# Retention's output products in high and low float32r parts, its gated product on VectorE, and convolution taps moved to a later stage

## The chip, the cores and the metric

One core of a Trainium2 chip runs the whole program. The metric is the device time in microseconds of one execution, as the median of several runs. The engines have short names in the profile: PE is TensorE (matmuls), PEld its weight loads, DVE VectorE, ACT ScalarE, POOL GpSimd, SP the engine that issues most transfers.

## The reference, cut to what matters

Three mixers follow each other over 256 tokens of width 1024: a gated delta rule, a short convolution, and a third block. The third block projects its normed input by one wide matrix into queries and keys (1024 each), values and a gate (2048 each), and the inputs of a convolution of width 31. What this case touches, in float32:

```python
# retention, per head h of 4 (dk 256, dv 512), chunks of 128 tokens
scores = einsum('bhid,bhjd->bhij', qc, kc) * decay_mask
inner  = einsum('bhij,bhje->bhie', scores, vc)
...
ret = head_groupnorm(retention_chunkwise(qh, kh, vh)).reshape(B, S, RET_V_DIM)
y_a = (ret * silu(z_ret)) @ w_ret_out
a = u_val * sigmoid(u_gate)
a = causal_depthwise_conv_2(a, conv_w, conv_b)      # 31 taps
a = silu(layernorm(a, conv_ln_g, conv_ln_b))
y_b = (a * silu(z_conv)) @ w_conv_out
merged = sigmoid(g_a) * y_a + sigmoid(g_b) * y_b
```

With 256 tokens there are two chunks, and the kernel computes the second chunk's sum over both chunks' keys directly, without a state.

## The kernel before

**Stages.** The program is one chain of projections, each cut into chunks of 256 weight columns (PHASES): ... qk (8 chunks), v (8), zret (8, the retention's gate), zconv (4), gates (8), ret_out (8), conv_out (4), w_out (4). A weight chunk of 128x2048 float32 is loaded into one of four raw slots; ScalarE writes its high part (w_hi, float32r, in halves of 128x1024), VectorE the rest (w_lo = raw - w_hi), and TensorE multiplies high x high, high x low and low x high (wide_half, L727, L728 and L734: eight matmuls with w_hi, then four with w_lo per half, of 512 columns each). There are four places for halves of w_hi and w_lo, so a half can be split only when TensorE has finished the half that stood there four halves earlier.

**Who does what beside.** Each engine has one fixed program order. For each chunk VectorE first does two low splits (second half of the next chunk, first half of the one after), then what `each` gives it: a number of convolution taps (conv_share, instructions of 128x256, L2399, L2396 for a first tap), and the work of the stage. There are 8 x 31 = 248 taps; conv_share takes from a list in order and does nothing when the list is empty. The conv_share counts for each chunk are written by hand.

- glu: 3, 4, 5, 4, 2, 4 taps from chunk 2 on; qk: 3 for each chunk.
- v: TensorE computes one head's scores after each of the first four chunks (`scores`, L1134); VectorE multiplies them with the decay into st (L2459); ScalarE copies v out of PSUM after each second chunk (vt, L1641).
- zret: after each chunk TensorE computes one output block of 128 tokens x 512 from st and vt (`weighted_sums`, L1146, and L1148 for the second chunk of tokens), as float32 matmuls. VectorE takes statistics from it (L2477, L2481); ScalarE the root (L1656) and then the normed output og (L1662). GpSimd multiplies og with the silu of the gate, back into vt (L1773).
- zconv: TensorE transposes the product (`turn_two`, L1160), ScalarE and VectorE write its high and low parts (yT_hi, yT_lo).
- gates: ScalarE takes sigmoids (L1641). VectorE has taps and, behind them in its last chunk, two sums of the convolved channels for the layer norm's mean (L2502, L2506). GpSimd makes two sums before those (L1777, and L1780, which waits for cv_step of 186 taps).
- ret_out: after its first chunk TensorE waits for those sums (`layer_norm`, ln_sum_step of 4) and multiplies them with ones (L1169). VectorE and ScalarE do the norm beside the later chunks.

Of the kernel before, what the change touches and what calls it, by code (L numbers as in the profile page):

```python
# [53 lines left out]
PHASES = [("qkv", 16), ("z", 8), ("gdn_out", 8), ("sc_in", 32), ("sc_out", 8), ("glu", 8), ("qk", 8), ("v", 8),  # L54
          ("zret", 8), ("zconv", 4), ("gates", 8), ("ret_out", 8), ("conv_out", 4), ("w_out", 4)]
ORDER = [name for name, _ in PHASES]
READ_BY = {name: "act" if name in ("z", "v", "zret", "zconv", "gates") else "dve" for name in ORDER}
DEEP = ("gdn_out", "sc_out", "ret_out")
DEEP_NEXT = ("sc_in", "glu")
CW2 = 2 * CC  # L60
# [30 lines left out]
V_PRE, V_PRE2, V_BADA, V_CB, V_LG, V_LB, V_C, V_SC = 0, 16, 24, 48, 56, 64, 72, 80  # L91
ANGLE_STEPS = 12
SHIFTED = ((4, 5, 6, 7), (6, 7))
E_LEAST = 0.5 * math.log(RMS_EPS) - 0.1
EYE, T_SIDE, S_BASE = 3, 4, 5
G_ROW = 32
# [2 lines left out]
def build(nc, x_in, pre_norm_w, post_norm_w, gdn_w_in, gdn_conv_w, gdn_A_log, gdn_dt_bias, gdn_norm_w, gdn_w_out,  # L99
# [3 lines left out]
    with ctx:  # L103
# [123 lines left out]
        qkT = at("qkT", o_q, [P, 2 * KT, SEQ])  # L227
        vt = at("vt", o_q + 16 * K, [P, NT, 2 * D])
        o_t = o_q + 32 * K
        st = at("st", o_t, [P, RH, 3 * P])  # L230
        glu, rp1, rp2 = (at(n, o_t + 2 * s * K, [P, 2, SEQ]) for s, n in enumerate(("glu", "rp1", "rp2")))
        lnm = at("lnm", o_t + 7 * K, [P, 2, SEQ])
        cT_hi, cT_lo = at("cT_hi", o_ar, [P, KT, SEQ], F32R), at("cT_lo", o_q + 24 * K, [P, KT, SEQ], F32R)
# [16 lines left out]
        def bank(b, inner=SEQ):  # L250
# [64 lines left out]
        cv_step, mean_done, xc_ready, a2_ready, var_done, ln_step = (  # L315
            sem(n) for n in ("cv_step", "mean_done", "xc_ready", "a2_ready", "var_done", "ln_step"))
        lna_ready, lns_ready, lnz_ready = sem("lna_ready"), sem("lns_ready"), sem("lnz_ready")
        chi_ready, cop_ready, mg_ready, mhi_ready, mop_ready = (
            sem(n) for n in ("chi_ready", "cop_ready", "mg_ready", "mhi_ready", "mop_ready"))
        qs_done, o1_ready, gn_rec, ln_scalars = (  # L320
            sem(n) for n in ("qs_done", "o1_ready", "gn_rec", "ln_scalars"))
        mg_turned = sem("mg_turned")
# [256 lines left out]
        def _(pe):  # L579
# [558 lines left out]
            def weighted_sums(c):  # L1138

                h, t = c // NT, c % NT  # L1140
                pe.wait_ge(st_ready, min(RH, c + 1))
                if c >= 4:
                    pe.wait_ge(gn_ready, c - 3)
                vh = slice(h * RDV, (h + 1) * RDV)
                o = psum[:, 4 + c % 4, :]
                mm = pe.matmul(o, st[:, h, t * P:(t + 1) * P], vt[:, 0, vh], start=True, stop=(t == 0))  # L1146
                if t:
                    mm = pe.matmul(o, st[:, h, SEQ:SEQ + P], vt[:, 1, vh], start=False, stop=True)  # L1148
                mm.then_inc(ro_done, 1)
            wide_phase("zret", hT_hi, hT_lo, beside=weighted_sums)  # L1150

# [57 lines left out]
        def _(act):  # L1209
# [434 lines left out]
            def channels_out(dst, func):  # L1644
# [1 line left out]
                    act.wait_ge(half_done, done)  # L1646
                    act.activation(dst[:, bass.ds(i * 8 + 2 * j, 2), :], bank(j), func).then_inc(bank_free, 1)
                return each
            chunks("v", tokens_out(vt, ACT.Copy))
            z_ret = tokens_out(zr, ACT.Silu)  # L1650

            def group_norm(h):
# [36 lines left out]
            def layer_norm(i, j, done):  # L1689
                c = 4 * i + j  # L1690
                if c == 1:
                    for q in range(KT // 2):
                        pair = slice(2 * q, 2 * q + 2)
                        act.wait_ge(xc_ready, q + 1)
                        act.activation(a2[:, pair, :], cv[:, pair, :], ACT.Square).then_inc(a2_ready, 1)
                if c == 3:
                    act.wait_ge(var_done, 1)
                    act.activation(lnm[:, 1, :], psum[:, 7, 0:SEQ], ACT.Sqrt, scale=1.0 / D, bias=eps_n[:, :]).then_inc(ln_step, 1)
                if c in (4, 5):
                    for n in range(KH2 * (c - 4), KH2 * (c - 3)):  # L1700
                        act.wait_ge(lns_ready, n // 2 + 1)
                        act.activation(cv[:, n, :], cv[:, n, :], ACT.Silu, scale=par[:, 1, V_LG + n:V_LG + n + 1],
                                       bias=par[:, 1, V_LB + n:V_LB + n + 1]).then_inc(lna_ready, 1)
                if c in (5, 6):
                    for q in range(2 * (c - 5), 2 * (c - 4)):
                        pair = slice(2 * q, 2 * q + 2)
                        act.wait_ge(lnz_ready, q + 1)
                        act.activation(cT_hi[:, pair, :], cv[:, pair, :], ACT.Copy).then_inc(chi_ready, 1)
            chunks("ret_out", layer_norm, unroll=True)
            act.activation(warm[:, 1:2], eps_r[:, :], ACT.Sqrt)  # L1710

# [16 lines left out]
        @block.gpsimd  # L1728
        def _(pool):
            pool.memset(ba_raw[:, :, :], 0.0).then_inc(padded, 1)  # L1730
            pool.memset(Tq[:, :], 0.0).then_inc(filled, 1)
            pool.wait_ge(small_loaded, SMALL)
            pool.wait_ge(small_ready, 3)
            pool.tensor_scalar(keep[:, :], const[:, C_LOW, :], -1.0, 1.0, ALU.mult, ALU.add).then_inc(filled, 1)
            pool.wait_ge(filled, 1)
            pool.memset(Tq[:, 0:BS * BS:BS + 1], 1.0).then_inc(filled, 1)
            pool.wait_ge(filled, EYE)
            def mask(n):
                p, c = n // NT, n % NT
                mine = PT[:, c, HG * p:HG * (p + 1), :]  # L1740
                pool.wait_ge(pt_ready, n + 1)
                pool.tensor_tensor(mine, mine, heads(keep[:, :], HG), ALU.mult).then_inc(masked, 1)
            for n in range(LATE):
                mask(n)
            pool.wait_ge(l2_sum, KT)
            pool.wait_ge(qkv_ready, COUNT["qkv"])
            pool.memset(Tc[0:BS, :, BS:2 * BS], 0.0).then_inc(filled, 1)
            pool.wait_ge(ktok_ready, KT // 2)
            pool.memset(S[0], 0.0).then_inc(filled, 1)
            pool.wait_ge(lo_ready, 2 * (FIRST["z"] + 7))  # L1750
            pool.memset(S[1], 0.0).then_inc(filled, 1)
            pool.wait_ge(eg_ready, 1)
            pool.wait_ge(ktok_ready, KT // 2)
            for p in range(NPAIR):
                for n in {0: (4, 5), 1: (6, 7)}.get(p, ()):
                    mask(n)
                if p == 0:
                    pool.wait_ge(half_done, 4 + 2 * FIRST["gdn_out"])
                else:
                    pool.wait_ge(s1_done, p)  # L1760
                for a in range(HG):
                    h = HG * p + a
                    i = pool.tensor_scalar(kdec[:, a, :], ktok[:, h // 2, :], wdec[:, h:h + 1], None, ALU.mult)
                i.then_inc(kdec_ready, 1)

            pool.wait_ge(yT_turned, KT)
            pool.memset(ada_sum[:, :, :], 0.0).then_inc(ada_used, ADA)

            for n in range(NT * RH):
                h, t = n // NT, n % NT  # L1770
                pool.wait_ge(gn_ready, n + 1)
                vh = slice(h * RDV, (h + 1) * RDV)
                pool.tensor_tensor(vt[:, t, vh], og[t][:, :], zr[:, t, vh], ALU.mult).then_inc(rg_ready, 1)  # L1773

            pool.wait_ge(rg_ready, NT * RH)
            pool.wait_ge(cv_step, CW * 4)
            pool.tensor_tensor(ln_sum[0][:, :, :], cv[:, 0:2, :], cv[:, 2:4, :], ALU.add).then_inc(ln_sum_step, 1)  # L1777
            pool.wait_ge(ln_sum_step, 1)
            pool.wait_ge(cv_step, CW * 6)
            pool.tensor_tensor(ln_sum[0][:, :, :], ln_sum[0][:, :, :], cv[:, 4:6, :], ALU.add).then_inc(ln_sum_step, 1)  # L1780
# [3 lines left out]
        def _(dve):  # L1784
# [668 lines left out]

            def decayed(i, j, done):
                c = 4 * i + j
                conv_share(9 if c < RH else 8)
                if c < RH:
                    dve.wait_ge(sco_done, c + 1)
                    dve.tensor_tensor(st[:, c, :], psum[:, 4 + c, 0:3 * P], decay[:, c, :], ALU.mult).then_inc(st_ready, 1)  # L2459
            dve.wait_ge(decay_loaded, 16)  # L2460
            dve.wait_ge(bank_free, 4 + FIRST["v"])
            chunks("v", decayed, unroll=True)

            def group_scale(h):
# [2 lines left out]
                dve.wait_ge(gn_rec, 2 * h + 1)  # L2467
                dve.scalar_tensor_tensor(out=gnm[:, :], in0=gmv[:, :, 0], scalar=-1.0, in1=grs[:, :], op0=ALU.mult, op1=ALU.mult).then_inc(gn_rec, 1)

            def group_norm(i, j, done):  # L2470
                n = 4 * i + j
                h, t = n // NT, n % NT
                if n and t == 0:
                    group_scale(h - 1)
                conv_share(7)
                dve.wait_ge(ro_done, n + 1)
                dve.bn_stats(gst[:, t, :], psum[:, 4 + n % 4, :]).then_inc(gn_step, 1)  # L2477
                dve.wait_ge(gn_step, 2 * n + 1)
                if h:
                    dve.wait_ge(gn_rec, 2 * h)  # L2480
                dve.bn_aggr(gmv[:, t, :], gst[:, t, :]).then_inc(gn_step, 1)  # L2481
            chunks("zret", group_norm, unroll=True)

            def turned_pairs(i, j, done):
                if j == 0:
                    group_scale(RH - 1)
                conv_share(5 if j else 8)
                split_two(j)

            def split_two(q):  # L2490
# [26 lines left out]
            def layer_norm(i, j, done):  # L2517
# [27 lines left out]
                if c in (6, 7):  # L2545
                    for q in range(2 * (c - 6), 2 * (c - 5)):
                        pair = pairs[q]
                        dve.wait_ge(chi_ready, q + 1)
                        part_lo(cT_lo[:, pair, :], cv[:, pair, :], cT_hi[:, pair, :]).then_inc(cop_ready, 1)
                if j == 3:  # L2550
                    dve.wait_ge(half_done, done)
# [85 lines left out]
```

## Time and profile before

| | |
|---|---|
| median of 3 runs | 838.21 us (837.5 to 838.33) |
| profiled execution, own time | 837.87 us |
| its span, first to last instruction | 836.1 us |
| PE busy | 827.8 us (99%) |
| DVE busy | 731.1 us (87%) |
| ACT busy | 500.2 us (60%) |
| POOL busy | 45.4 us (5%) |

Read it so: the share of an engine says how much of the span it has an instruction at work. Starts in a timeline are microseconds from the start of the span. Matmuls are pipelined, so the distance of two starts, not the duration, is what one costs.

### The profile page before, as it was taken

The numbers are of one execution on the slowest core, as the hardware profiler recorded it, in microseconds if no ns is written. First come the engines' busy times: TensorE is split into PE (matmuls) and PEld (weight loads), VectorE is DVE, ScalarE is ACT, GpSimd is POOL, SyncE is SP. The second block draws the span as 40 slices with busy tenths as digits, with TensorE's granted clock in tenths as the row PEclk, the third lists the DMA queues.
The fourth block names the chain that finished last, engine by engine and source line by source line (L and its number), as shares of the span: only waits on it lengthen the run. The fifth ranks groups of instructions, "written<-read, shape, count | busy, mean of one in ns | idle before, by whom it ended". The sixth has DMA issues, their size and how long they took to land.

```text
span 836.1 us, 13942 instructions
## 1 busy us (share of the span) xinstructions
PE 827.8 (99%) x5146; PEld 725.1 (87%) x5146; DVE 731.1 (87%) x1179; ACT 500.2 (60%) x804; POOL 45.4 (5%) x46
## 2 busy tenths in 40 slices
PE   8999999999999999999999999999999999999997
PEld 8999998789888888888888788998887798888886
DVE  7799899868877898888989979999999999988774
ACT  6899858576566555555565775333346675546743
POOL 0001101341100000000000000000001220000000
PEclk9999999999999999999999999999999999999999
DMA  9875675511875877777776656655454435564531
GB/s 277 256 253 169 211 245 174 146 38 45 278 232 179 261 262 263 257 256 252 238 257 218 221 185 213 202 184 169 155 198 151 152 118 200 186 231 171 188 115 50
DMA packets 129882, 164.13 MB, mean 196 GB/s; under 512 B 17407, under 2 KB 92199, under 8 KB 129703
## 3 DMA queue, kind: packets, MB, share of 16 engines
q1 hardware_dynamic: 129831, 163.45, 59.9%
q8 instruction: 33, 0.54, 0.3%
q14 instruction: 18, 0.15, 0.1%
HBM read 159.20 MB, written 4.23 MB: 195 GB/s over the span
## 4 chain that ended last, share of the span: by engine, by line
PE 98%; DVE 1%; DMA 1%; issue 0%; ACT 0%; DVEq 0%; SPq 0%; ACTq 0%
PE psum L695 16%; PE psum L727 14%; PE psum L728 14%; PE psum L734 14%; PE psum L704 8%; PE psum L677 6%; PE psum L686 6%; PE psum L678 6%; PE psum L1028 2%; PE psum L631 1%; PE psum L641 1%; PE psum L635 1%; PE psum L1033 1%; PE psum L915 1%; PE psum L1146 1%; PE psum L1134 1%
## 5 line engine op out<-in xcount | busy, mean ns | idle before, releaser
L1220 ACT ACTIVATE w_hi<-w_raw 128x1024 fp32r<-128x1024 f32 x255 | 266.6, 1061 | 188.2 <-PE psum L734 87.1
L1786 DVE TENSOR_TENSOR w_lo<-w_raw,w_hi 128x1024 fp32r<-128x1024 f32 x256 | 305.2, 1221 | 44.3 <-ACT w_hi L1220 42.2
L695 PE MATMUL psum<-hT,w_hi 128*128 128x512 f32 x576 | 138.9, 391 | 0.0
L695 PEld LDWEIGHTS psum<-hT,w_hi 128*128 128x128 f32 x576 | 105.4, 188 | 20.2
L727 PE MATMUL psum<-w_hi,hT 128*128 128x512 f32 x280 | 113.3, 405 | 0.0
L728 PE MATMUL psum<-w_hi,hT 128*128 128x512 f32 x280 | 109.3, 390 | 0.0
L2399 DVE SCALAR_TENSOR_TENSOR cv<-aP,par,cv 128x256 f32<-128x256 f32 x240 | 107.9, 519 | 0.0
L677 PE MATMUL psum<-hT,w_hi 128*128 128x256 f32 x432 | 107.4, 286 | 0.0
L678 PE MATMUL psum<-hT,w_hi 128*128 128x256 f32 x432 | 105.9, 283 | 0.0
L677 PEld LDWEIGHTS psum<-hT,w_hi 128*128 128x128 f32 x432 | 82.8, 192 | 0.4 <-issue 0.2
L678 PEld LDWEIGHTS psum<-hT,w_hi 128*128 128x128 f32 x432 | 82.9, 192 | 0.3 <-issue 0.2
L704 PEld LDWEIGHTS psum<-hT,w_lo 128*128 128x128 f32 x576 | 74.8, 191 | 3.3
L704 PE MATMUL psum<-hT,w_lo 128*128 128x256 f32 x576 | 76.1, 283 | 0.0
L727 PE MATMUL psum<-w_hi,yT_hi 128*128 128x512 f32 x192 | 75.8, 395 | 0.0
L734 PE MATMUL psum<-w_lo,hT 128*128 128x512 f32 x280 | 75.6, 390 | 0.0
L728 PE MATMUL psum<-w_hi,yT_lo 128*128 128x512 f32 x192 | 74.8, 390 | 0.0
L727 PEld LDWEIGHTS psum<-w_hi,hT 128*128 128x128 f32 x280 | 52.6, 188 | 12.0 <-issue 1.7
L728 PEld LDWEIGHTS psum<-w_hi,hT 128*128 128x128 f32 x280 | 52.6, 188 | 12.0 <-issue 1.7
L734 PEld LDWEIGHTS psum<-w_lo,hT 128*128 128x128 f32 x280 | 52.6, 188 | 11.2
L686 PE MATMUL psum<-hT,w_lo 128*128 128x256 f32 x432 | 60.6, 283 | 0.0
L686 PEld LDWEIGHTS psum<-hT,w_lo 128*128 128x128 f32 x432 | 55.7, 192 | 0.0
L734 PE MATMUL psum<-w_lo,yT_hi 128*128 128x512 f32 x192 | 52.7, 389 | 0.0
(341 smaller groups left out, 1108.6 us busy)
## 6 DMA issues: line engine op xcount, KB each, us to landing
w_raw<-in_w_in_dram SPq DMA_DIRECT2D x44, 1024.0 KB, 5.1
w_raw<-in_sc_w_in_dram SPq DMA_DIRECT2D x32, 1024.0 KB, 7.9
w_raw<-in_gdn_w_in_dram SPq DMA_DIRECT2D x23, 1024.0 KB, 7.1
ada<-in_w_ada_dram SPq DMA_DIRECT2D x24, 512.0 KB, 4.8
w_raw<-in_gdn_w_out_dram SPq DMA_DIRECT2D x8, 1024.0 KB, 5.5
w_raw<-in_sc_w_out_dram SPq DMA_DIRECT2D x8, 1024.0 KB, 6.4
w_raw<-in_w_ret_out_dram SPq DMA_DIRECT2D x8, 1024.0 KB, 5.1
w_raw<-in_w_conv_out_dram SPq DMA_DIRECT2D x4, 1024.0 KB, 5.1
```

What stands on the lines that cost most here:

```text
L677: pe.matmul(o[:, m, :], w_hi[s][:, k, mine], a_hi[:, ka, :], start=m == 0 and ka == 0, stop=False, skip_group_check=True)
L678: pe.matmul(o[:, m, :], w_hi[s][:, k, mine], a_lo[:, ka, :], start=False, stop=False, skip_group_check=True)
L686: mm = pe.matmul(o[:, m, :], w_lo[s][:, k, mine], a_hi[:, ka, :], start=False, stop=ka == KT - 1, skip_group_check=True)
L695: pe.matmul(o, w_hi[s][:, k, mine], hT[:, h * KH2 + k, :, :], start=h == 0 and k == 0, stop=False, skip_group_check=True)
L704: mm = pe.matmul(o, w_lo[s][:, k, mine], hT_hi[:, ka, :], start=False, stop=ka == KT - 1, skip_group_check=True)
L727: pe.matmul(psum[:, b + m, :], a_hi[:, ka, mine], wide(w_hi[s])[:, e, :], start=start and h == 0 and e == 0, stop=False, skip_group_check= ...
L728: pe.matmul(psum[:, b + m, :], a_lo[:, ka, mine], wide(w_hi[s])[:, e, :], start=False, stop=False, skip_group_check=True)
L734: mm = pe.matmul(psum[:, b + m, :], a_hi[:, k + 2 * h + e, mine], wide(w_lo[s])[:, e, :], start=False, stop=stop and h == 1 and e == 1, sk ...
L1028: mm = pe.matmul(b[:, a, :], left(a), right(a), start=True, stop=True)
L1220: act.activation((w_hi[half_slot(g, h)] if home is None else third_hi[half_slot(g, home)])[:, :, :], raw[slot][:, h * KH2:(h + 1) * KH2, : ...
L1786: return dve.tensor_tensor(o, whole, hi.bitcast(F32), ALU.subtract)
L2399: dve.scalar_tensor_tensor(out=cv[:, n, :], in0=src, scalar=w, in1=cv[:, n, :], op0=ALU.mult, op1=ALU.add).then_inc(cv_step, 1)
```

## The change

TensorE's output products use st and vt as high and low float32r parts, three products in place of one float32 product. In v, ScalarE writes the high parts of vt (from PSUM) and of st, VectorE the low ones, and VectorE frees v's banks. VectorE, not GpSimd, multiplies og with the gate (`gated`), one head late in program order. Taps: in v from 9 and 8 for each chunk to 8, then 6, 6, 6 and 7; in zret from 7 to 6. conv_share in gates is as before: 4 for chunk 0, 10 for each other. The semaphore chi_ready is renamed part_hi_ready and counts these parts first.

```diff
-READ_BY = {name: "act" if name in ("z", "v", "zret", "zconv", "gates") else "dve" for name in ORDER}
+READ_BY = {name: "act" if name in ("z", "zret", "zconv", "gates") else "dve" for name in ORDER}
+PARTS_BY = [sum((d >= RH) + d % 2 for d in range(c + 1)) for c in range(COUNT["v"])]
...
+        vt_hi, vt_lo = at("vt_hi", o_q + 16 * K, [P, NT, 2 * D], F32R), at("vt_lo", o_yT + 16 * K, [P, NT, 2 * D], F32R)
+        st_hi, st_lo = (at(n, o_q + 6 * s * K, [P, RH, 3 * P], F32R) for s, n in enumerate(("st_hi", "st_lo")))
...
             def weighted_sums(c):
-                pe.wait_ge(st_ready, min(RH, c + 1))
+                pe.wait_ge(st_ready, RH + h + 1)
...
-                mm = pe.matmul(o, st[:, h, t * P:(t + 1) * P], vt[:, 0, vh], start=True, stop=(t == 0))
-                if t:
-                    mm = pe.matmul(o, st[:, h, SEQ:SEQ + P], vt[:, 1, vh], start=False, stop=True)
+                for b in range(t + 1):
+                    cs = slice(t * P, (t + 1) * P) if b == 0 else slice(SEQ, SEQ + P)
+                    pe.matmul(o, st_hi[:, h, cs], vt_hi[:, b, vh], start=b == 0, stop=False, skip_group_check=True)
+                    pe.matmul(o, st_hi[:, h, cs], vt_lo[:, b, vh], start=False, stop=False, skip_group_check=True)
+                    mm = pe.matmul(o, st_lo[:, h, cs], vt_hi[:, b, vh], start=False, stop=b == t, skip_group_check=True)
...
# ScalarE
-            chunks("v", tokens_out(vt, ACT.Copy))
+            def beside_v(i, j, done):
+                c = 4 * i + j
+                if c >= RH:
+                    act.wait_ge(st_ready, RH)
+                    act.wait_ge(sco_done, RH)
+                    act.activation(st_hi[:, c - RH, :], st[:, c - RH, :], ACT.Copy).then_inc(part_hi_ready, 1)
+                if c % 2:
+                    act.wait_ge(half_done, done)
+                    act.activation(vt_hi[:, :, c // 2 * CW2:(c // 2 + 1) * CW2], psum[:, j - 1:j + 1, :], ACT.Copy).then_inc(part_hi_ready, 1)
+            chunks("v", beside_v, unroll=True)
...
# GpSimd
-            for n in range(NT * RH):
-                h, t = n // NT, n % NT
-                pool.wait_ge(gn_ready, n + 1)
-                vh = slice(h * RDV, (h + 1) * RDV)
-                pool.tensor_tensor(vt[:, t, vh], og[t][:, :], zr[:, t, vh], ALU.mult).then_inc(rg_ready, 1)
...
# VectorE, v
-                conv_share(9 if c < RH else 8)
+                conv_share(8 if c < RH else 6 + c // 7)
...
+                else:
+                    dve.wait_ge(part_hi_ready, PARTS_BY[c - 1] + 1)
+                    part_lo(st_lo[:, c - RH, :], st[:, c - RH, :], st_hi[:, c - RH, :]).then_inc(st_ready, 1)
+                if c % 2:
+                    dve.wait_ge(part_hi_ready, PARTS_BY[c])
+                    columns = slice(c // 2 * CW2, (c // 2 + 1) * CW2)
+                    part_lo(vt_lo[:, :, columns], psum[:, j - 1:j + 1, :], vt_hi[:, :, columns]).then_inc(bank_free, 2)
...
# VectorE, zret and zconv
+            def gated(h):
+                vh = slice(h * RDV, (h + 1) * RDV)
+                for t in range(NT):
+                    dve.wait_ge(gn_ready, NT * h + t + 1)
+                    dve.tensor_tensor(vt[:, t, vh], og[t][:, :], zr[:, t, vh], ALU.mult).then_inc(rg_ready, 1)
...
-                conv_share(7)
+                conv_share(6)
...
+                if n and t == 0:
+                    gated(h - 1)
...
                 conv_share(5 if j else 8)
+                if j == 0:
+                    gated(RH - 1)
                 split_two(j)
```

## Rows read from the trace of the kernel before

**Rows 1.** Page, busy us, share of the span, instructions.
```profile
PE 827.8 (99%) x5146; PEld 725.1 (87%) x5146; DVE 731.1 (87%) x1179; ACT 500.2 (60%) x804; POOL 45.4 (5%) x46
```

**Rows 2.** Page, chain that ended last, shares by engine.
```profile
PE 98%; DVE 1%; DMA 1%; issue 0%; ACT 0%; DVEq 0%; SPq 0%; ACTq 0%
```

**Rows 3.** Busy time in stretches: v, zconv, gates.
```profile
core 0: us, PE busy (x) PEld busy (x) DVE busy (x) ACT busy (x) POOL busy (x), PEclk, DMA share, GB/s
567.40:616.60 49.20, 49.20 (x228) 41.08 (x227) 47.34 (x88) 19.73 (x19) 0.00 (x0) 1.00 0.53 171
...
670.80:697.20 26.40, 26.40 (x226) 26.40 (x224) 26.33 (x43) 18.25 (x25) 5.57 (x4) 1.00 0.49 160
697.20:740.80 43.60, 43.60 (x195) 36.12 (x193) 43.60 (x80) 21.76 (x22) 0.00 (x0) 1.00 0.52 170
```

**Rows 4.** Timeline of PE in zret: start us, us, engine, line, operation.
```profile
622.05 1.02 PE L1146 MATMUL psum<-vt,st 128*128 128x512 f32 x2
...
625.67 0.39 PE L727 MATMUL psum<-w_hi,hT 128*128 128x512 f32 x1
...
628.40 1.02 PE L1146 MATMUL psum<-vt,st 128*128 128x512 f32 x2
...
632.88 0.39 PE L727 MATMUL psum<-w_hi,hT 128*128 128x512 f32 x1
```

**Rows 5.** Timeline of DVE: decay multiply in v, first part of zret.
```profile
576.37 0.55 DVE L2459 TENSOR_TENSOR st<-psum,decay 128x384 f32<-128x384 f32 x1
...
619.49 2.41 DVE L1786 TENSOR_TENSOR w_lo<-w_raw,w_hi 128x1024 fp32r<-128x1024 f32 x2
```

**Rows 6.** Timeline of POOL: one pair of multiplies, second layer-norm sum.
```profile
637.10 2.88 POOL L1773 TENSOR_TENSOR vt<-og,zr 128x512 f32<-128x512 f32 x2 [415.67 <-ACT og L1662]
...
694.84 1.33 POOL L1780 TENSOR_TENSOR ln_sum<-ln_sum,cv 128x512 f32<-128x512 f32 x1 [11.33 <-DVE cv L2399]
```

**Rows 7.** Timeline of DVE: taps and splits in zret, a product in ret_out.
```profile
636.12 4.94 DVE L2399 SCALAR_TENSOR_TENSOR cv<-aP,par,cv 128x256 f32<-128x256 f32 x7
...
641.80 2.33 DVE L1786 TENSOR_TENSOR w_lo<-w_raw,w_hi 128x1024 fp32r<-128x1024 f32 x2
644.04 2.85 DVE L2399 SCALAR_TENSOR_TENSOR cv<-aP,par,cv 128x256 f32<-128x256 f32 x7
...
655.83 2.33 DVE L1786 TENSOR_TENSOR w_lo<-w_raw,w_hi 128x1024 fp32r<-128x1024 f32 x2
...
776.60 1.29 DVE L2544 TENSOR_TENSOR cv<-cv,zc 128x512 f32<-128x512 f32 x2
```

**Rows 8.** Timeline of DVE in gates, from its part for chunk 1 on.
```profile
706.74 2.35 DVE L1786 TENSOR_TENSOR w_lo<-w_raw,w_hi 128x1024 fp32r<-128x1024 f32 x2
709.01 4.04 DVE L2399 SCALAR_TENSOR_TENSOR cv<-aP,par,cv 128x256 f32<-128x256 f32 x10
...
737.87 2.37 DVE L1786 TENSOR_TENSOR w_lo<-w_raw,w_hi 128x1024 fp32r<-128x1024 f32 x2
...
742.81 0.70 DVE L2502 TENSOR_TENSOR ln_sum<-ln_sum,cv 128x512 f32<-128x512 f32 x1
743.54 0.42 DVE L2506 TENSOR_TENSOR ln_sum<-ln_sum 128x256 f32<-128x256 f32 x1
```

**Rows 9.** Timeline of PE: chunk 1 of gates, its second half, the mean matmul.
```profile
702.74 0.39 PE L727 MATMUL psum<-w_hi,hT 128*128 128x512 f32 x1
...
705.46 0.39 PE L727 MATMUL psum<-w_hi,hT 128*128 128x512 f32 x1
...
746.26 0.59 PE L1169 MATMUL psum<-ln_sum,const 128*128 128x256 f32 x2
```

**Rows 10.** Timeline of ACT in gates.
```profile
705.72 1.06 ACT L1220 ACTIVATE w_hi<-w_raw 128x1024 fp32r<-128x1024 f32 x1 [1.72 <-PE psum L734]
```

**Rows 11.** Stretches behind the last matmul, columns as in rows 3.
```profile
831.00:832.00 1.00, 0.14 (x2) 0.00 (x0) 1.00 (x4) 0.77 (x3) 0.00 (x0) 1.00 0.46 174
...
834.00:834.50 0.50, 0.00 (x0) 0.00 (x0) 0.00 (x0) 0.00 (x0) 0.00 (x0) 0.52 0.98 365
```

More of the change, by code:

```diff
@@ L317, in build @@
         lna_ready, lns_ready, lnz_ready = sem("lna_ready"), sem("lns_ready"), sem("lnz_ready")
-        chi_ready, cop_ready, mg_ready, mhi_ready, mop_ready = (
-            sem(n) for n in ("chi_ready", "cop_ready", "mg_ready", "mhi_ready", "mop_ready"))
+        part_hi_ready, cop_ready, mg_ready, mhi_ready, mop_ready = (
+            sem(n) for n in ("part_hi_ready", "cop_ready", "mg_ready", "mhi_ready", "mop_ready"))
         qs_done, o1_ready, gn_rec, ln_scalars = (
@@ L1707, in layer_norm @@
                         act.wait_ge(lnz_ready, q + 1)
-                        act.activation(cT_hi[:, pair, :], cv[:, pair, :], ACT.Copy).then_inc(chi_ready, 1)
+                        act.activation(cT_hi[:, pair, :], cv[:, pair, :], ACT.Copy).then_inc(part_hi_ready, 1)
             chunks("ret_out", layer_norm, unroll=True)
@@ L2547, in layer_norm @@
                         pair = pairs[q]
-                        dve.wait_ge(chi_ready, q + 1)
+                        dve.wait_ge(part_hi_ready, 2 * RH + q + 1)
                         part_lo(cT_lo[:, pair, :], cv[:, pair, :], cT_hi[:, pair, :]).then_inc(cop_ready, 1)
```

## The prediction, made before the change was run

> **What bounds the kernel now.** I read the page's busy times first: the matmuls cover 99% of the span [rows 1]. The chain that ended last says the same: 98% of it is PE [rows 2]. So only two things can move the time: matmul work that is taken off TensorE, and a wait that TensorE does not have today. The table by stage shows no PE idle in v (from 567.4), zconv and gates (to 740.8), at a granted clock of 1.00, its 2.4 GHz level, while VectorE (DVE) is full too in zconv and gates: 26.33 of 26.40 us and 43.60 of 43.60 [rows 3]. The timelines of single engines then show how late DVE runs behind PE, and where. That distance decides this case. I call the start of DVE's part for a chunk minus PE's start of that chunk its lag.
>
> **What the change takes from TensorE.** Today each of the 12 output products is a full float32 matmul, recorded as two. A weight half of 12 matmuls takes 628.40 - 625.67 = 2.73 us, 0.2275 each; with one float32 product it takes 625.67 - 622.05 = 3.62, with two 632.88 - 628.40 = 4.48 [rows 4]. So a head (three products) costs 0.89 + 1.75 = 2.64 us, four heads 10.56. Afterwards a head is nine high/low products of the same shape and kind as the weight matmuls: 9 x 0.2275 = 2.05, four heads 8.19. TensorE gains 2.4 us, all on the chain. Nothing else on TensorE changes. Bounds of this term: 2.3 by the dearer pair alone (12 x (0.875 - 0.6825)) and 2.5 by the single (12 x (0.89 - 0.6825)).
>
> **The v stage.** ScalarE's copy of v stays and writes the high part; it gets four more copies, of 128x384. A copy of 1024 columns takes it 1.06 us [rows 10], so one of 384 less than that, and it idles 29 of the 49 us there [rows 3]: no cost. DVE gets four st_lo (128x384, priced as today's decay multiply, 0.55 long and some 0.46 from start to next start [rows 5]) and four vt_lo (128x1024, one input in PSUM; priced as a weight split of that shape, 1.14 from start to next start [rows 8]; a PSUM input may make it dearer or cheaper by a tenth, within the lag's reserve below), 6.4 us in all, and loses 11 taps of 0.396 [rows 8], 4.4 us. Its lag at the end of v, 619.49 - 616.6 = 2.9 today [rows 5], grows to about 4.4 us. What hides this: each DVE part begins with the low half that PE wants 5.44 + 2.72 + 1.82 = 9.98 us after the chunk's start, and the split takes 1.2, so PE waits only once the lag passes 8.8 (the three terms are a chunk, a half and eight matmuls of [rows 4]). The banks of v are freed by DVE instead of ScalarE, a few us later, but PE comes back to a pair only a pair of chunks (over 10 us) afterwards. What the first product newly waits for, st_lo of head 0, is written in DVE's part for chunk 4 of v, four chunks before PE reaches it at 622.05 [rows 4]. No PE wait here; if the cover were gone, each us would count in full.
>
> **zret and zconv.** GpSimd's eight multiplies go. While a pair of them runs (2.88 us from 637.10), seven DVE taps take 4.94 us in place of 2.85 [rows 6, 7]: 2.09 us lost, four times, 8.4 in all. DVE now does the multiplies itself: 128x512 with both inputs in SBUF, two in 1.29 [rows 7], 4.9 in all, and 8 taps (3.2) leave. The Trainium skill (GPSIMD Engine Reference, Key points) says that GpSimd shares its SBUF interfaces with VectorE and that instructions with two SBUF inputs contend; the 4.94 against 2.85 agrees. By rows a pair of DVE parts costs 655.83 - 641.80 = 14.03 today [rows 7] and 14.03 - 2.09 - 0.79 + 1.22 = 12.4 after, against 13.52 - 0.6 = 12.9 for PE. So DVE, which falls behind today, catches up, down to the least lag that the weight slots allow. In zconv its part (8 or 5 taps as today) is 5.45 against 6.6 for PE, so it catches up there as well. Today its lag at chunk 1 of gates is 706.74 - 702.74 = 4.0 [rows 8, 9]; by this walk it is at the least that the slots allow. This gain cannot reach PE: PE waits for none of it.
>
> **gates: where the taps land.** The shares must add up to 248 taps (8 blocks of channels, 31 taps). Before: 22 (glu) + 24 (qk) + 68 (v) + 56 + 23 leaves 55 for gates: 4, five times 10, 1, 0. After: 22 + 24 + 57 + 48 + 23 leaves 74: 4 and seven times 10. So chunks 6 and 7 of gates, in which DVE recovers today, are full. A part with 10 taps takes 6.23 us (706.74 to 737.87 is five of them) [rows 8]; PE's chunk takes 5.44. And behind the last tap stand the two sums of the layer norm (742.81 to 743.96, 1.15 us), for which PE waits after the first chunk of ret_out. Today they are ready 2.3 us before PE reaches that matmul at 746.26 [rows 8, 9].
>
> Step by step, with PE 2.4 us earlier. PE starts chunk 1 of gates at 702.74 - 2.4 = 700.35. The second split in DVE's part for it needs ScalarE's high copy, which needs the slot of PE's half (today PE 705.46, copy 705.72 to 706.78) [rows 9, 10]; so it starts at 704.4 at the earliest, however early DVE is. Plus 1.14 and 3.95 for ten taps: 709.5. GpSimd's second layer-norm sum waits for tap 186, which is now the eighth of this part. It lasts 1.33 us [rows 6], and a multiply pair of 2.88 costs DVE 2.09, 73% of its length: +1.0, 710.5. Six more parts of 6.23: 747.9. The two sums: 749.0. PE arrives at 746.26 - 2.4 = 743.9 and waits **5.2 us**. It goes on at 749.1, where today it goes on at 746.26: **+2.8 us**. All behind it (the rest of ret_out, conv_out, w_out) is PE-bound and shifts with it. Before the wait, the lag at chunk 7 is 741.6 - 733.0 = 8.6, just inside 8.8, so a low half may hold PE for a few tenths already; that would be part of the same 5.2. Bounds: if GpSimd's sum pushes nothing and the slots hold nothing back, DVE's work alone gives 700.35 + 1.2 + 7 x 6.23 + 1.15 = 746.3, no change at all. If DVE enters with today's lag of 4.0 at chunk 1, 700.35 + 4.0 + 43.6 + 1.15 + 1.0 = 750.1, +3.8.
>
> **The clock behind the wait.** After its last matmul (end 831.14) TensorE is idle and the granted clock goes from 1.00 to 0.50, which is 1.2 GHz, at 834.0, 2.9 us later [rows 11]. A wait of 5.2 us is longer than that. No row shows how long it then stays down once work resumes. Below: no cost, if it does not fall. Above: it stays down for a whole chunk's work, 5.44 us lost. I take the time it took to fall, 2.9 us at half speed, as an estimate: 1.45 us lost. The Trainium skill (TensorE: Matmul & The Clock Gate, Part 1) states that an idle array goes to the lower clock and needs sustained work to return; the tail agrees on the fall, and no run here shows the return.
>
> **The cases.** The sum is made on the profiled execution, span 836.1, own time 837.87; the median of the runs is 838.21, 0.3 above it, and I add differences to the median.
> - Late sums, clock falls: 838.2 + 2.8 + 1.45 = **842.5**. Chance 0.49.
> - Late sums, clock holds (the fall may also come later than in the tail): 841.0 (to 842.0 with the larger lag). Chance 0.31.
> - Rival on the other side, the sums are not late: 838.2 - 2.4 = 835.8. It decides if DVE is done by 743.9. For it: DVE gets 3.5 us back in zret and zconv. Against it: those us end at the slot limit, and even at the bound DVE ends at 746.3; its parts in gates would have to be 5 us cheaper than the rows. Chance 0.06.
> - The two cancel, at the bound of no push and no hold: 838.2. Chance 0.06.
> - DVE is later than walked, because the new steps of v and zret (low parts waiting for ScalarE, multiplies waiting for the normed output) add to the lag, or the clock stays low for long: about 845 or more. Chance 0.08.
>
> A measurement of this kernel tells about 0.2% (1.7 us) from no change. The range 840.0 to 844.5 holds the first two cases, 0.8. Faster 0.06, same 0.07 (the cancelling case and the edge of the second), slower 0.87.
>
> **What the profile after would show.** Right: 36 products at 0.23 us, zret shorter by 2.4; groups of taps in zret no longer stretched; seven parts of 6.23 us back to back in gates; a PE wait of about 5 us on DVE's ln_sum in front of the layer norm's mean matmul, and granted clock under 1.00 around it. Wrong: no PE wait there (then the tap or split price or the count of taps is off), or a PE wait on w_lo, on a bank in v, or on st_lo. A stall of the right size with the clock at 1.00 would take away the 1.45.

## The result: 0.6% slower, and the profile after

The changed kernel takes 843.0 us (median, 842.28 to 844.61) against 838.17 for the one before: a ratio of 1.0061, 95% interval 1.0048 to 1.0074. The execution shown below took 844.11 us itself, 1.1 above its median, with a span of 842.3 against 836.1. This is the page's chain of work that ended last, which answers to [rows 2]:

```profile
PE 83%; DVE 9%; DMA 3%; issue 2%; ACT 1%; SPq 0%; DVEq 0%; ACTq 0%
```

PE had 98% of it before. Now DVE has 9%. Some 5 of these 9 are the 44.6 us from 705.16 to 749.76 in gates, where the chain runs through DVE's splits and taps. Nearly all of the rest, and of DMA's 3%, lies before 440 us, in sc_out and ahead of it: the chain gets there through the small wait of L730 below, and that has nothing to do with the change. Who waited for whom on PE (us in total, times, longest) names the place:

```profile
PE psum L1174 <- DVE ln_sum L2532: 5.0, 1, 5.0
...
PE psum L730 <- ACT w_hi L1225: 0.3, 1, 0.3
```

L1174 is the matmul for the layer norm's mean. The first row did not exist before. The second is a weight half that came late in sc_out, long before the changed stages, in this execution; the kernel of the seventh experiment shows such a row too (0.5) and the first experiment's does not.

PE's timeline, first an output product of zret (answers to [rows 4]), then the place of the wait (answers to [rows 9]):

```profile
622.89 0.39 PE L1151 MATMUL psum<-vt_hi,st_hi 128*128 128x512 f32 x1
623.12 0.39 PE L1152 MATMUL psum<-vt_lo,st_hi 128*128 128x512 f32 x1
623.35 0.39 PE L1153 MATMUL psum<-vt_hi,st_lo 128*128 128x512 f32 x1
623.57 0.39 PE L730 MATMUL psum<-w_hi,hT 128*128 128x512 f32 x1
...
743.70 1.07 PE L737 MATMUL psum<-w_lo,yT_hi 128*128 128x512 f32 x4
749.81 1.22 PE L1174 MATMUL psum<-ln_sum,const 128*128 128x256 f32 x2 [5.04 <-DVE ln_sum L2532]
750.47 0.99 PE L730 MATMUL psum<-w_hi,yT_hi 128*128 128x512 f32 x1
751.26 0.63 PE L731 MATMUL psum<-w_hi,yT_lo 128*128 128x512 f32 x1
751.68 0.63 PE L730 MATMUL psum<-w_hi,yT_hi 128*128 128x512 f32 x1
...
755.69 0.40 PE L730 MATMUL psum<-w_hi,yT_hi 128*128 128x512 f32 x1
```

Three products start 0.227 us apart, in 0.68 us together. PE would start the mean matmul at 743.70 + 4 x 0.227 = 744.61. It starts 5.20 us later, and then matmuls of 512 columns follow at 0.43 us instead of 0.23 until 755.69. From the first output product to the point where PE reaches the mean matmul it is 744.61 - 622.89 = 121.72 us, before 746.26 - 622.05 = 124.21 [rows 4, 9]: TensorE did gain 2.49 us.

DVE's timeline in gates (answers to [rows 8]):

```profile
705.16 1.23 DVE L1795 TENSOR_TENSOR w_lo<-w_raw,w_hi 128x1024 fp32r<-128x1024 f32 x1 [1.49 <-ACT w_hi L1225]
706.30 3.25 DVE L2408 SCALAR_TENSOR_TENSOR cv<-aP,par,cv 128x256 f32<-128x256 f32 x8
709.47 1.71 DVE L2405 TENSOR_SCALAR cv<-aP,par 128x256 f32<-128x256 f32 x2
711.10 2.35 DVE L1795 TENSOR_TENSOR w_lo<-w_raw,w_hi 128x1024 fp32r<-128x1024 f32 x2
...
742.26 2.35 DVE L1795 TENSOR_TENSOR w_lo<-w_raw,w_hi 128x1024 fp32r<-128x1024 f32 x2
744.54 4.03 DVE L2408 SCALAR_TENSOR_TENSOR cv<-aP,par,cv 128x256 f32<-128x256 f32 x10
748.61 0.69 DVE L2528 TENSOR_TENSOR ln_sum<-ln_sum,cv 128x512 f32<-128x512 f32 x1
749.33 0.43 DVE L2532 TENSOR_TENSOR ln_sum<-ln_sum 128x256 f32<-128x256 f32 x1
```

Read it from the top. In its part for chunk 1 DVE idles 1.49 us for ScalarE's high copy: it is not behind here, it is held. From 705.16 on it never idles again. The row of L2405 holds two taps; GpSimd's second sum (1.33 us from 709.69) runs beside them and stretches them. Five parts take 742.26 - 711.10 = 31.16 us, 6.23 each; the last ten taps and the sums end at 749.76, and PE goes on at 749.81.

Busy time by stretch around the wait (columns as in [rows 3]; the figure behind POOL's is the granted clock):

```profile
747.00:748.00 1.00, 0.00 (x0) 0.00 (x0) 1.00 (x3) 0.00 (x0) 0.00 (x0) 1.00 1.01 393
748.00:749.00 1.00, 0.00 (x0) 0.00 (x0) 0.97 (x3) 0.00 (x0) 0.00 (x0) 0.76 0.11 43
...
754.00:755.00 1.00, 1.00 (x4) 0.81 (x3) 0.00 (x0) 0.00 (x0) 0.00 (x0) 0.50 1.04 403
755.00:756.00 1.00, 1.00 (x5) 0.77 (x5) 0.00 (x0) 0.05 (x1) 0.00 (x0) 0.83 1.06 371
```

The clock is at 0.50 (1.2 GHz) from about 748.5 to about 755.3 (0.76 is about half of its stretch, 0.83 two thirds of one). Work at that level from 749.81 to 755.3 loses half of 5.5 us, 2.75. The timeline agrees: from the mean matmul to the next half it is 755.69 - 749.81 = 5.88 us, and in the kernel before 749.46 - 746.26 = 3.20, 2.7 less. The difference of the two spans then comes out: -2.49 (products) + 0.84 (PE reaches the first product at 622.89, not 622.05) + 5.20 (the wait) + about 2.7 (the clock) = 6.2, and 842.3 - 836.1 is 6.2. The 0.84 is there before v begins (PE starts v at 568.47, not 567.62), ahead of everything that was changed. It belongs to these two executions: the medians differ by 4.8, and less the 5.20 - 2.49 = 2.7 of wait and products that leaves 2.1 us for the clock.

### The profile page after: what moved, and what is told of

It is laid out like the page before. It is cut to its first block, busy times and chain, and to the rows that moved or that the text cites. A ratio compares the mean times of both kernels' runs of the same rounds, so it can differ in the third digit from the quotient of the medians.

```text
span 842.3 us, 13964 instructions
## 1 busy us (share of the span) xinstructions
PE 828.6 (98%) x5158; PEld 728.9 (87%) x5158; DVE 732.8 (87%) x1195; ACT 502.0 (60%) x808; POOL 33.8 (4%) x38
## 4 chain that ended last, share of the span: by engine, by line
PE 83%; DVE 9%; DMA 3%; issue 2%; ACT 1%; SPq 0%; DVEq 0%; ACTq 0%
PE psum L730 12%; PE psum L731 12%; PE psum L737 12%; PE psum L698 10%; PE psum L680 6%; PE psum L689 6%; PE psum L681 6%; PE psum L707 5%; DVE cv L2408 3%; DMA w_raw<-in_sc_w_in_dram 3%; DVE w_lo L1795 3%; PE psum L1031 2%; DVE ada_sum L2281 1%; PE psum L634 1%; PE psum L644 1%
## 5 line engine op out<-in xcount | busy, mean ns | idle before, releaser
L730 PE MATMUL psum<-w_hi,hT 128*128 128x512 f32 x280 | 110.4, 394 | 0.0
L731 PE MATMUL psum<-w_hi,hT 128*128 128x512 f32 x280 | 109.2, 390 | 0.0
L2408 DVE SCALAR_TENSOR_TENSOR cv<-aP,par,cv 128x256 f32<-128x256 f32 x240 | 98.5, 475 | 0.0
L730 PE MATMUL psum<-w_hi,yT_hi 128*128 128x512 f32 x192 | 77.0, 401 | 0.3 <-ACT w_hi L1225 0.3
L730 PEld LDWEIGHTS psum<-w_hi,hT 128*128 128x128 f32 x280 | 52.6, 188 | 10.5
```

The lines of the kernel that those rows point to most:

```text
L730: pe.matmul(psum[:, b + m, :], a_hi[:, ka, mine], wide(w_hi[s])[:, e, :], start=start and h == 0 and e == 0, stop=False, skip_group_check= ...
L731: pe.matmul(psum[:, b + m, :], a_lo[:, ka, mine], wide(w_hi[s])[:, e, :], start=False, stop=False, skip_group_check=True)
L2408: dve.scalar_tensor_tensor(out=cv[:, n, :], in0=src, scalar=w, in1=cv[:, n, :], op0=ALU.mult, op1=ALU.add).then_inc(cv_step, 1)
```

## The experiments

Experiments 1 to 4 ask where the 5 us come from and what the clock costs, 5 to 8 take single terms, 9 asks whether a shorter wait still costs clock. The theory: all of the slowdown is the 19 taps that landed in gates, through the wait for the sums and the clock behind it. The main rival: the new steps (low parts, products on VectorE, another owner of v's banks) make it.

**1. The changed kernel with the old tap counts.**

```diff
-                conv_share(8 if c < RH else 6 + c // 7)
+                conv_share(9 if c < RH else 8)
...
-                conv_share(6)
+                conv_share(7)
```

> The changed kernel with the tap counts of before: 9 and 8 in v, 7 in zret, so that 55 taps are left for gates and the last two chunks of gates are free again. Theory (the taps in gates make VectorE late for the layer-norm sums): no wait in front of the mean matmul, granted clock 1.00 up to the tail, only TensorE's 2.5 us gain is left: 835.7 us, 7.3 below the changed kernel. VectorE's new low parts and products then push its lag in v and zret up to about 8 us, close to the 8.8 at which TensorE would wait for w_lo, so a few tenths may be lost. Rival (the slowdown comes from the new steps themselves, the low parts, the products on VectorE, the changed owner of v's banks): still 840 or more, with the wait on w_lo or on a bank.

Measured: 835.38 us, ratio to before 0.996 (0.9948 to 0.9972). The wait is gone, the clock stays. DVE's sums in this kernel:

```profile
741.05 0.68 DVE L2528 TENSOR_TENSOR ln_sum<-ln_sum,cv 128x512 f32<-128x512 f32 x1
741.77 0.42 DVE L2532 TENSOR_TENSOR ln_sum<-ln_sum 128x256 f32<-128x256 f32 x1
```

and PE's matmul behind them:

```profile
743.64 0.62 PE L737 MATMUL psum<-w_lo,yT_hi 128*128 128x512 f32 x2
744.10 0.59 PE L1174 MATMUL psum<-ln_sum,const 128*128 128x256 f32 x2
```

The sums are ready at 742.19, 1.9 us early. All new steps are in this kernel and it is faster than before: the rival falls, and with it every story in which low parts or v's banks cost time here.

**2. The kernel before with the new tap counts alone.** The same two lines, the other way round, in the kernel before.

> The kernel before with only the new tap counts (8, then 6, 6, 6, 7 in v; 6 in zret), all else as before. Theory: VectorE's part for chunk 1 of gates is held by the weight slots just as in the changed kernel, so the sums come some 5 us after TensorE, the clock falls, and nothing is gained on TensorE: 838.2 + 5.1 + about 2.6 = 845.9 us, with one PE wait of about 5 us in front of the mean matmul. Rival (the new steps make VectorE late, the counts alone do not): within 0.3% of before, 838 to 840.

Measured: 845.34 us, ratio 1.0076 (1.0059 to 1.0092). The wait is there without any of the new steps:

```profile
753.22 1.22 PE L1169 MATMUL psum<-ln_sum,const 128*128 128x256 f32 x2 [5.02 <-DVE ln_sum L2506]
```

The counts alone cost 7.3 us (before is 838.05 in this comparison); less the products' 2.5 us gain, this is the changed kernel's +4.8. The clock is at 0.50 from 752.2 to 759.0 in the profiled execution.

**3. Work in place of idling.** 20 matmuls (FILL is 20) into an unread bank in front of the wait; they add work and change nothing that is computed.

```diff
                 if c == 0:
+                    pe.wait_ge(y_op_ready, 3 * KT)
+                    for r in range(FILL):
+                        pe.matmul(psum[:, 4, :], yT_hi[:, r % 8, 0:P], yT_hi[:, 8 + r % 4 * 2:10 + r % 4 * 2, :], start=True, stop=True)
                     pe.wait_ge(ln_sum_step, 4)
```

> The changed kernel with 20 extra matmuls of 512 columns (4.5 us of work, into a bank that is not read) in front of the wait for the layer-norm sums, so that TensorE is not idle for more than about 1 us. Theory (the fall of the clock behind the wait costs time of its own): the sums come at the same time, the clock stays at 1.00, and the matmuls behind run at 0.23 us from the first: 840.4 us, 2.6 below the changed kernel. Rival (the lower clock is a mark of the wait and costs nothing that the wait had not cost): no difference, 843.0.

Measured: 840.7 us. PE's timeline:

```profile
744.11 4.70 PE L1176 MATMUL psum<-yT_hi 128*128 128x512 f32 x20
749.32 0.70 PE L1178 MATMUL psum<-ln_sum,const 128*128 128x256 f32 x2 [0.52 <-DVE ln_sum L2536]
749.67 0.58 PE L731 MATMUL psum<-w_hi,yT_hi 128*128 128x512 f32 x1
750.09 0.39 PE L732 MATMUL psum<-w_hi,yT_lo 128*128 128x512 f32 x1
750.32 0.40 PE L731 MATMUL psum<-w_hi,yT_hi 128*128 128x512 f32 x1
```

The mean matmul still comes 5.2 us late, but behind it the matmuls run at 0.23 us. 843.0 - 840.7 = 2.3 us is what the clock costs in the medians (2.2 if each is taken against the runs of the kernel before beside it, 838.17 and 838.05). The rival, that it costs nothing of its own, falls.

**4. The mean matmul one chunk later.** `if c == 0:` becomes `if c == 1:` for the wait and the matmul.

> The changed kernel with the mean matmul and its wait one chunk of ret_out later (after chunk 1). Theory: TensorE reaches it 5.4 us later, about when the sums are ready, so the wait shrinks to under 1 us and the clock stays. But the next limits are near: VectorE then begins ret_out 10 us behind, over the 8.8 at which its low halves are late (some tenths to 1 us), and the variance matmul after chunk 3 has only about 0.1 us left of its reserve of 5.5. 836 to 838.5 us. Rival (VectorE's total lateness has to be paid anyway): 841 or more, the wait only changes its place.

Measured: 836.86 us, ratio 0.9989 (0.9979 to 0.9999), 6.1 below the changed kernel. No wait at the mean matmul is left; the next limit is the one that was named, though larger than the 1 us given:

```profile
750.05 1.20 PE L737 MATMUL psum<-w_lo,yT_hi 128*128 128x512 f32 x4 [1.65 <-DVE w_lo L1795]
```

The clock does not fall behind this wait:

```profile
750.00:751.00 1.00, 0.95 (x4) 0.82 (x5) 1.00 (x1) 0.00 (x0) 0.00 (x0) 1.00 0.00 0
751.00:752.00 1.00, 1.00 (x7) 0.81 (x6) 1.00 (x2) 0.00 (x0) 0.00 (x0) 1.00 0.37 70
```

VectorE's lateness did not have to be paid: most of it was paid only because the fixed order asked for the sums after the first chunk.

**5. The exchange of engines alone**, in the kernel before: GpSimd's loop out, `gated` in VectorE's order as in the change.

> The kernel before with one part of the change: VectorE multiplies the normed outputs with the gates, GpSimd does not; float32 products and the tap counts of before stay. Theory: VectorE gains some 3.5 us in zret and zconv, its taps there are no longer stretched from 2.85 to 4.94 us, but TensorE waits for none of it today: 838.0 us, no change that can be measured. Rival (the swap itself costs, since the products come later in program order and the transposes of zconv wait): 839 or more with a PE wait in zconv.

Measured: 837.98 us, no difference (ratio 1.0005, 0.9995 to 1.0014). The taps beside the products:

```profile
635.94 2.85 DVE L2394 SCALAR_TENSOR_TENSOR cv<-aP,par,cv 128x256 f32<-128x256 f32 x7
...
639.54 1.26 DVE L2469 TENSOR_TENSOR vt<-og,zr 128x512 f32<-128x512 f32 x2
```

Seven taps take 2.85 us where they took 4.94 [rows 7]. VectorE gains, TensorE waits for none of it, and the time does not move.

**6. Experiment 1 with the products back on GpSimd**, so that high and low parts meet the stretched taps.

> The changed kernel with the tap counts of before (as in the first experiment) and the products back on GpSimd. Theory: VectorE loses 2.09 us to each pair of GpSimd products and is spared 1.2 of its own, 3.5 us in all; in the first experiment its lag was already near the 8.8 at which TensorE waits for w_lo, so now TensorE waits in zconv and at the end of gates, 1.5 to 2.5 us in all: 837 to 838 us, most of TensorE's gain lost again. Rival (the swap of engines is beside the point): 835.4, as in the first experiment.

Measured: 839.58 us, ratio 1.0021 (1.0012 to 1.003). The direction was right, the size not: 4.2 us are lost against experiment 1, not 2. Who waited, by the weight loads of PE:

```profile
PEld psum L689 <- DVE w_lo L1801: 1.7, 2, 1.3
PEld psum L737 <- DVE w_lo L1801: 1.4, 2, 0.9
...
PEld psum L1165 <- issue: 0.7, 2, 0.5
PEld psum L680 <- ACT w_hi L1225: 0.5, 1, 0.5
```

Those are 4.3 us, in zconv and at the end of gates, and PE's starts say the same: from the first output product to the first matmul of ret_out it is 743.08 - 622.64 = 120.44 us, in experiment 1 738.66 - 622.38 = 116.28, 4.2 less. Besides w_lo a transpose and a w_hi came late, which the expectation had left out. So the exchange that is worth nothing alone (5) is worth 4 us once the low parts have used up VectorE's room.

**7. The taps laid by room.**

```diff
-                conv_share(8 if c < RH else 6 + c // 7)
+                conv_share((8, 8, 8, 8, 7, 6, 7, 7)[c])
...
-                conv_share(6)
+                conv_share(7 - n % 2)
...
-                conv_share(5 if j else 8)
+                conv_share(7 if j else 9)
...
-                conv_share(10 if c else 4)
+                conv_share((6, 9, 9, 9, 9, 9, 9, 1)[c])
```

> The changed kernel with the taps laid where VectorE has room: 8, 8, 8, 8, 7, 6, 7, 7 in v, 7 and 6 in turn in zret, 9, 7, 7, 7 in zconv, and 6, six times 9 and 1 in gates. Theory: by the rows no lag passes 6 us and the sums are ready over 1 us before TensorE asks for them, so nothing but TensorE's 2.5 us gain shows: 835.5 us, the same as with the old counts (which already had no wait), only with more reserve. Rival (there is something left in the first experiment that the trace does not show): under 835.

Measured: 835.97 us, ratio 0.9973 (0.9963 to 0.9983); no wait on VectorE in the changed stages. It is not to be told from experiment 1: the intervals overlap. Either version beats the kernel before, by about the 2.5 us of the products (2.7 and 2.0 in the medians), and the changed kernel by 7 us or a little more.

**8. GpSimd's second sum cut to 4 of 256 tokens** (the rest of channels 512 to 767 is left out of the mean), in the changed kernel.

> The changed kernel with GpSimd's second layer-norm sum cut to 4 of 256 tokens (the other tokens of channels 512 to 767 are left out of the mean), so that it hardly uses the memory. Theory: this sum pushes VectorE's taps in chunk 1 of gates by 1.0 us, and all of it ends up in TensorE's wait: the wait shrinks from 5.0 to 4.0 us and the time to 842.0 us or a little less, if the clock still falls (if it does not, 839.3). Rival (the push falls into idle time of VectorE): 843.0 and a wait of 5.0.

Measured: 841.22 us, 1.8 below the changed kernel (1.6 if each is taken against the runs of the kernel before beside it). The two first taps beside GpSimd's sum are no longer stretched (0.73 us, 1.71 in the changed kernel), and the wait shrank by the 1.0 us that was foreseen:

```profile
708.60 0.73 DVE L2405 TENSOR_SCALAR cv<-aP,par 128x256 f32<-128x256 f32 x2
...
747.95 0.70 PE L1174 MATMUL psum<-ln_sum,const 128*128 128x256 f32 x2 [4.06 <-DVE ln_sum L2532]
```

In the profiled execution the clock is down for a shorter time as well, from about 749.1 to 752.6:

```profile
748.00:749.00 1.00, 1.00 (x5) 0.87 (x6) 1.00 (x2) 0.00 (x0) 0.00 (x0) 1.00 0.00 0
749.00:750.00 1.00, 1.00 (x4) 0.80 (x3) 1.00 (x2) 0.00 (x0) 0.00 (x0) 0.57 0.00 0
...
752.00:753.00 1.00, 1.00 (x4) 0.79 (x4) 0.00 (x0) 0.00 (x0) 0.00 (x0) 0.72 1.05 408
```

From the mean matmul to the next half it is 752.82 - 747.95 = 4.87 us, 1.0 less than in the changed kernel. That fits the rest of the gain; one profile does not prove it.

**9. A shorter filler**: experiment 3 with 9 matmuls.

> The changed kernel with only 9 extra matmuls of 512 columns (2.05 us) in front of the wait for the layer-norm sums, so that TensorE idles for about 3.1 us in place of 5.0. The clock fell 2.9 us (tail of the kernel before), 3.7 us (changed kernel) and 4.0 us (tap counts alone) after the last matmul, and even in the run whose wait was 4.1 us. Theory (the fall follows the length of the idle time): at 3.1 us it stays at 1.00 in most executions or falls only for a moment: 840.5 to 841.5 us. Rival (any wait of some us costs the fall, since the lower clock comes with a delay even after work has begun again): 843.0.

Measured: 842.47 us. The theory fell. PE idled 3.0 us, and the clock was still at 1.00 when it went on; then

```profile
749.17 0.70 PE L1178 MATMUL psum<-ln_sum,const 128*128 128x256 f32 x2 [3.01 <-DVE ln_sum L2536]
749.52 0.58 PE L731 MATMUL psum<-w_hi,yT_hi 128*128 128x512 f32 x1
749.94 0.39 PE L732 MATMUL psum<-w_hi,yT_lo 128*128 128x512 f32 x1
750.17 0.50 PE L731 MATMUL psum<-w_hi,yT_hi 128*128 128x512 f32 x1
750.46 0.63 PE L732 MATMUL psum<-w_hi,yT_lo 128*128 128x512 f32 x1
```

the matmuls lengthen from 0.39 to 0.63 us after about 1 us of work. The granted clock falls there and comes back some 3.4 us later:

```profile
750.00:751.00 1.00, 1.00 (x5) 0.76 (x4) 1.00 (x2) 0.00 (x0) 0.00 (x0) 0.66 0.00 0
...
753.00:754.00 1.00, 1.00 (x4) 0.85 (x3) 0.00 (x0) 0.00 (x0) 0.00 (x0) 0.64 1.05 410
```

From the mean matmul to the next half it is 754.05 - 749.17 = 4.88 us, against 752.62 - 749.32 = 3.30 in experiment 3 and 5.88 in the changed kernel. So the fall cost 1.6 us here: the rival is right that it is paid, but in this execution it is not the same price as behind 5.0 us. Waits of 0.5 us (experiment 3) and 1.65 us (experiment 4) brought no fall; what lies between 1.65 and 3.0 us was not tried.

## Why the prediction was right, point by point

The forecast was 842.5 us with a range of 840.0 to 844.5; 843.0 was measured. Its likeliest case, late sums and a fallen clock, is what the trace shows.

- **TensorE's gain, 2.4 us:** 2.49, in the changed kernel and, from 622.38 to 744.10, in experiment 1.
- **v, zret, zconv without a wait:** so in the trace; waits there appear only in experiment 6, once the stretched taps are added. VectorE did catch up and was held at chunk 1 of gates, by 1.49 us. Two small slips did no harm. The lag at the end of v should have been 2.9 + 6.4 - 4.4 = 4.9 by the forecast's own terms, not 4.4; it measured 622.10 - 617.45 = 4.65. And 5.45 us holds for the parts of zconv with 5 taps; the one with 8 taps took 680.82 - 672.02 = 8.80. The low part of v out of PSUM, priced as a weight split of 1.14 us, took 1.13 (620.97 to 622.10).
- **The walk through gates:** the second split of chunk 1 was put at 704.4 and came at 705.16, PE being some 0.8 us later in this execution. From there to the end of the sums 44.6 us were forecast and 749.76 - 705.16 = 44.6 measured. The lag at chunk 7 was put at 8.6, inside the 8.8; it was 742.26 - 733.73 = 8.53, and no low half held PE.
- **GpSimd's push, 1.0 us:** two first taps took 1.71 us, 0.73 in experiment 8, where the wait shrank by 1.0.
- **The wait, 5.2 us:** 5.20. Its cause is shown from both sides: counts back, wait gone (1); counts alone, wait there (2).
- **The clock, 1.45 us:** right in kind, too small in size. It measured 2.3 us in the medians (3) and about 2.7 in the profile. The estimate assumed that the clock stays down as long as it took to fall, 2.9 us; it stayed down for 5.5 us of work. No row stood behind that assumption, as the forecast itself says; that it came this near owes something to luck. This term alone was short by 0.7 us (2.1 left by the medians) to 1.2 (the profile), more than the 0.5 us by which the whole forecast was low; 2.8 for wait less products against 2.7 measured gave 0.1 of it back.
- **The rivals:** that the sums would not be late is what experiments 1 and 7 measure, 835.4 and 836.0; the forecast had 835.8 for it. The cancelling case did not occur, since VectorE was held at chunk 1 and pushed by GpSimd. The case of a clock that holds did not occur either.

The Trainium skill (GPSIMD Engine Reference, Key points) names the contention between GpSimd and instructions of VectorE with two SBUF inputs; experiment 5 agrees, 2.85 us in place of 4.94 for seven taps. By these rows VectorE lost 2.09 us beside 2.88 us of GpSimd.

## What to carry to other kernels

When work of a secondary engine is moved to a later stage, add it up to the first instruction of the bottleneck engine that needs it, not to the end of the stage. Here a part of gates with ten taps takes VectorE 6.23 us and TensorE's chunk 5.44, so that seven such parts in a row brought the sums 5 us late. An engine that is ahead cannot bank its lead if ring slots hold it back, so what is freed in an early stage does not pay for what is added in a later one. A wait of TensorE can cost more than its length: behind waits of 3.0 to 5.0 us the lower clock cost 1.6 to 2.7 us more here, behind one of 1.65 us nothing.

## What the runs showed of the hardware that was not expected

How long the clock stayed down, and when it fell, differed between these waits. Behind the two of 5.0 us (changed kernel, experiment 2) it fell while TensorE was still idle, 3.7 and 4.0 us after the last matmul, and stayed down for 6.8 us (748.5 to 755.3, 752.2 to 759.0). The stretches of experiment 2:

```profile
752.00:753.00 1.00, 0.00 (x0) 0.00 (x0) 0.95 (x2) 0.00 (x0) 0.00 (x0) 0.58 0.00 0
...
758.00:759.00 1.00, 1.00 (x4) 0.73 (x3) 0.00 (x0) 0.00 (x0) 0.00 (x0) 0.51 1.08 418
```

Behind the waits of 4.1 us (experiment 8) and 3.0 us (experiment 9) TensorE went on at 1.00, and the clock fell only after some 1.2 us of new work; it stayed down for about 3.4 us (749.1 to 752.6, 750.3 to 753.7). These are four profiled executions, one of each kernel: whether the length of the wait decides this, or when in the execution it falls, is not shown.
